# Chunk products of an mLSTM from fp32r high and low parts in place of plain fp32

## The chip, the cores and the metric

One core of one Trainium2 chip. The time is device microseconds (us) of one execution of the whole layer. The engines are called PE (TensorE), ACT (ScalarE), DVE (VectorE), POOL (GpSimd) and SP (SyncE, which issues nearly all DMAs).

## What is computed

A hybrid layer on 1024 tokens of width 1024, all in fp32: RMS norm, one wide input projection, a causal convolution, an mLSTM branch (4 heads of 256, chunks of 128 tokens), a dilated attention branch, two output projections with gates, a last projection and norm. The change is in the mLSTM recurrence, which per head and chunk of 128 tokens is

```python
C_new = decay * C + einsum('lk,lv->kv', w * k, v)        # state, 256 x 256
n_new = decay * n + einsum('lk->k', w * k)
s = einsum('ld,sd->ls', q, k) * exp(log_d - m_t)          # scores of the chunk
num = inter * (q @ C_prev) + s @ v
den = inter * (q @ n_prev) + s.sum(-1)
h = num / maximum(abs(den), exp(-m_t))
```

and in the sums that make the input and forget gates (`if_pre`) from the normed x.

## The kernel before, in words

The projections dominate. They are done by a seven-product scheme of Strassen's kind on blocks of x (B11, B21, B22 and the sums T1 to T4) and of the weights; each product is 4 contraction tiles times 3 matmuls, because every fp32 operand is split into an fp32r high part (hi, a rounded copy) and a low part (lo, the rest), and hi*hi, hi*lo and lo*hi are added in PSUM. One product is thus 12 matmuls of 128x512. The program is a hand-written table over steps k = 0, 1, ...; in step k PE does the side work of `items[k]`, then product k. For product k+3 the high part of the weights is made by ACT in step k (`high`, L1456; it waits until product k-1 is done) and the low part by POOL (`low`, L1080), or by DVE for two of seven products (L1887). POOL also makes the sums S1 and S2 of the weights (L1068, L1074) in every seventh step, after which S2 waits for a low part of DVE. DVE and ACT read the products out of PSUM and do the convolution ("taps", L2001, three per tile). Work of a step that comes behind `low` stands in the lists `act_late`, `dve_late`, `pool_late`; each engine works strictly in the order of its program.

The recurrence is side work of PE. Chunk (h, n) is number n of head h. Its start, in items[s] (`chunk_start`), makes the scores (L1317), turns the output gate (L1321), and turns k and v into the PSUM tile `keep` (L1332, L1334). ACT copies v and k (scaled) to `vv` and `kw` (L1721, L1723) and takes the exponential of the decay matrix `dmat` (L1726); DVE multiplies it with the scores into `w` (L2165). Its end, in items[s+2] (`chunk_end`), is up to five fp32 products of 258 columns: A = q times state (two, L1345; not for n = 0), B = w times v (L1350), C = k times v (two, L1354; not for n = 7). DVE then adds A and B, normalises, and updates `state` (L2190). The starts are at step 177 + 3.25 n for head 0, 203 + 4.375 n and 238 + 4.375 n for heads 1 and 2, and 273 + 3.5 n for head 3, rounded down. `keep` and the tiles of PSUM called side are read by order of semaphores; `pe_ring` counts the fills of the side ring.

At the start of the program x comes in eight row tiles; ACT squares five of them (L1508), POOL takes the root (L1092), DVE scales (L2076), PE turns them, ACT makes high parts (L1513) and DVE low parts (L2046) of B11 and B21. The gate sums are two side items: half 0 of the tokens from B11 and B21 (16 matmuls of 128x512 by L1259), half 1 from B11, T1 and B22 (24).

Of the kernel before, what the change touches and what calls it, by code (L numbers as in the profile page):

```python
# [13 lines left out]
P = 128  # L14
DM = 1024
# [26 lines left out]
HM_SLOTS = 12  # L42
# [103 lines left out]
def hybrid_kernel(nc, x, w_in, w_if, w_pm, w_pa, w_out, b_gate, conv_wt, conv_bt, pre_wt, m_wt, post_w,  # L146
# [94 lines left out]
    chunks = sorted(start_of, key=lambda c: start_of[c])  # L241
    for h, n in chunks:
        s = start_of[h, n]
# [100 lines left out]
    for s in range(NSTEP):  # L344
        for it in items[s]:
            what = it[0]
            if what == "if":
                fill(("if", it[1]), "act")
# [50 lines left out]
    with ctx:  # L399
# [65 lines left out]
        hm_sb = at("hm_sb", [P, HM_SLOTS, MD], F32, A_Q)  # L465
# [7 lines left out]

        state = small("state", [P, 2, VE], F32)
        kw_sb = [small(f"kw{i}", [P, MD], F32) for i in range(2)]
        vv_sb = [small(f"vv{i}", [P, VE], F32) for i in range(2)]
        w_sb = [small(f"w{i}", [P, P], F32) for i in range(2)]
        o_gate = [small(f"o_gate{i}", [P, MD], F32) for i in range(2)]
        dmat = small("dmat", [P, P], F32)
        total = small("total", [P, VE], F32)  # L480
        sq_junk = small("sq_junk", [P, MD], BF16, 2)
# [47 lines left out]
        ifw = small("ifw", [P, KT, 2 * MH], F32)  # L529
        assert pos[0] <= nc.sbuf_usable_end, (pos[0], nc.sbuf_usable_end)  # L530
# [51 lines left out]
        x2_in = [sem(f"x2_in{i}") for i in range(4)]  # L582
# [7 lines left out]
        pe_y = sem("pe_y")  # L590

        x_sq = sem("x_sq")
# [6 lines left out]
        ring_act = sem("ring_act")  # L599
        keep_act = sem("keep_act")  # L600
# [5 lines left out]
        e_done, kv_done, sq_done = sem("e_done"), sem("kv_done"), sem("sq_done")  # L606
        m_norm = sem("m_norm")
        att_hi, hm_hi, w_out_hi = sem("att_hi"), sem("hm_hi"), sem("w_out_hi")
        ysq_done, mg_hi = sem("ysq_done"), sem("mg_hi")

        v_step = sem("v_step")
        x_ms, x_sq_late, x_scaled = sem("x_ms"), sem("x_sq_late"), sem("x_scaled")
# [160 lines left out]
        def _(sp):  # L773
# [95 lines left out]
            def piece(it):  # L869
# [9 lines left out]
                elif what == "if_out":  # L879
                    ring_taken(sp, ("if", 1))  # L880
# [152 lines left out]
            def x_again(t):  # L1033
# [4 lines left out]
                sp.dma_start(gst[t % 4][:], x[t * P:(t + 1) * P, :]).then_inc(x2_in[t % 4], 16)  # L1038
# [19 lines left out]
        def _(g):  # L1058
# [28 lines left out]
            def reciprocal_root(t):  # L1087
                if t < 5:
                    g.wait_ge(x_ms, t + 1)
                else:  # L1090
                    g.wait_ge(x_sq_late, t - 4)
                TT(ssq[:, NT + t:NT + t + 1], ssq[:, t:t + 1], halfneg[:, 0:1], ALU.pow).then_inc(x_rs, 1)  # L1092

            def diagonal(t):
                reciprocal_root(t)
                g.wait_ge(x_rs, t + 1)
# [6 lines left out]
            for t in range(4):  # L1103
                reciprocal_root(t)
            reciprocal_root(4)
            low(0)
# [13 lines left out]
            for k in range(NSTEP):  # L1120
# [1190 lines left out]
```

## Time and profile before

| | |
|---|---|
| median of 3 runs | 1369.98 us (1368.76 to 1371.14) |
| the profiled execution | 1369.94 us, its span 1368.1 us |
| PE busy | 1352.3 us, 99% of the span |
| DVE, ACT, POOL busy | 794.5, 641.7, 569.2 us (58, 47, 42%) |
| PE's share of the chain that ended last | 91% |

The busy times of matmuls overlap (a record lasts longer than the distance to the next), so the cost of a matmul on PE is read from start to start in the order of time. A plain fp32 product is two records; an fp32r product, or a transpose, is one.

### The profile page before, as it was taken

How to read it: one execution, taken by the hardware profiler on the slowest of the kernel's cores; microseconds unless marked ns; L12 is line 12 of the kernel's file. 1: busy time of each engine (PE TensorE's matmuls, PEld its weight loads, DVE VectorE, ACT ScalarE, POOL GpSimd, SP SyncE). 2: the span in 40 equal slices, each digit the busy share in tenths (PEclk: the TensorE clock that was granted, in tenths of full speed). 3: DMA queues.
4: the chain of work that ended last, by engine and by line, in shares of the span. 5: the costliest groups of instructions: out<-in, count | busy, mean ns of one | idle time of the engine just before them, and what ended most of it. 6: DMA issues, size and time to landing. Idle time of an engine off the chain costs nothing.

```text
span 1368.1 us, 18779 instructions
## 1 busy us (share of the span) xinstructions
PE 1352.3 (99%) x6470; PEld 1127.3 (82%) x6470; DVE 794.5 (58%) x1260; ACT 641.7 (47%) x1320; POOL 569.2 (42%) x400
## 2 busy tenths in 40 slices
PE   7999999999999999999999999999999999999998
PEld 5788888888888888888888888888888888888786
DVE  5874438346543835877756575755644442997632
ACT  6644543543444455345445445544544553533421
POOL 5253435335443534654434445344333544454000
PEclk9999999999999999999999999999999999999999
DMA  6132233324233323455442634345343354966421
GB/s 194 51 76 65 69 74 90 96 48 126 76 85 72 84 79 61 149 173 144 114 145 66 188 104 134 100 127 175 87 150 97 93 188 165 345 200 196 183 97 58
DMA packets 210462, 165.02 MB, mean 121 GB/s; under 512 B 32400, under 2 KB 186544, under 8 KB 210368
## 3 DMA queue, kind: packets, MB, share of 16 engines
q1 hardware_dynamic: 210224, 163.75, 40.5%
q8 instruction: 53, 0.87, 0.3%
q14 instruction: 41, 0.34, 0.1%
q10 hardware_dynamic: 144, 0.07, 0.0%
HBM read 117.41 MB, written 40.08 MB: 115 GB/s over the span
## 4 chain that ended last, share of the span: by engine, by line
PE 91%; DVE 4%; issue 2%; ACT 1%; DMA 1%; SPq 1%; POOL 0%; DVEq 0%; POOLq 0%; ACTq 0%
PE proj L1244 69%; PE side L1189 3%; PE proj L1189 2%; PE side L1289 2%; PE side L1268 2%; PE side L1345 2%; PE side L1354 2%; PE proj L1170 2%; PE side L1170 2%; PE side L1277 1%; PE side L1317 1%; PE side L1350 1%; PE side L1300 1%; DMA x_sb<-x_in 1%; PE side L1362 1%
## 5 line engine op out<-in xcount | busy, mean ns | idle before, releaser
L1080 POOL TENSOR_TENSOR w_lo<-raw,w_hi 128x512 fp32r<-128x512 f32 x161 | 234.5, 1458 | 413.8 <-ACT w_hi L1456 413.7
L1244 PE MATMUL proj<-hi_T,w_hi 128*128 128x512 f32 x832 | 338.1, 406 | 2.2 <-ACT snap L1474 1.6
L1244 PE MATMUL proj<-hi_T,w_lo 128*128 128x512 f32 x832 | 325.2, 391 | 0.0
L1244 PE MATMUL proj<-lo_T,w_hi 128*128 128x512 f32 x832 | 324.1, 390 | 0.0
L1244 PE MATMUL proj<-hi_B,w_hi 128*128 128x512 f32 x624 | 254.1, 407 | 5.6 <-ACT b_sb L1518 4.0
L1244 PE MATMUL proj<-hi_B,w_lo 128*128 128x512 f32 x624 | 244.2, 391 | 0.0
L1244 PE MATMUL proj<-lo_B,w_hi 128*128 128x512 f32 x624 | 243.6, 390 | 0.0
L1080 POOL TENSOR_TENSOR w_lo<-s_sb,w_hi 128x512 fp32r<-128x512 f32 x104 | 156.7, 1510 | 153.5 <-ACT w_hi L1456 153.4
L1244 PEld LDWEIGHTS proj<-hi_T,w_hi 128*128 128x128 f32 x832 | 156.4, 188 | 36.0 <-issue 3.5
L1244 PEld LDWEIGHTS proj<-hi_T,w_lo 128*128 128x128 f32 x832 | 156.1, 188 | 34.2
L1244 PEld LDWEIGHTS proj<-lo_T,w_hi 128*128 128x128 f32 x832 | 156.6, 188 | 30.4
L1456 ACT ACTIVATE w_hi<-raw 128x512 fp32r<-128x512 f32 x216 | 135.2, 627 | 70.5 <-PE proj L1244 57.6
L1244 PEld LDWEIGHTS proj<-hi_B,w_hi 128*128 128x128 f32 x624 | 117.7, 189 | 29.9 <-ACT b_sb L1518 4.2
L1244 PEld LDWEIGHTS proj<-hi_B,w_lo 128*128 128x128 f32 x624 | 117.4, 188 | 25.4
L1244 PEld LDWEIGHTS proj<-lo_B,w_hi 128*128 128x128 f32 x624 | 117.8, 189 | 22.8
L1074 POOL TENSOR_TENSOR s_sb<-s_sb,raw 128x512 f32<-128x512 f32 x52 | 82.9, 1594 | 91.3 <-DVE w_lo L1887 90.5
L1456 ACT ACTIVATE w_hi<-s_sb 128x512 fp32r<-128x512 f32 x156 | 97.7, 627 | 37.9 <-PE proj L1244 28.9
L1887 DVE TENSOR_TENSOR w_lo<-s_sb,w_hi 128x512 fp32r<-128x512 f32 x52 | 43.9, 845 | 85.5 <-ACT w_hi L1456 85.5
L1068 POOL TENSOR_TENSOR s_sb<-raw 128x512 f32<-128x512 f32 x52 | 75.5, 1453 | 21.5 <-DVE w_lo L1887 21.4
L2001 DVE SCALAR_TENSOR_TENSOR tmp<-stage,cw,tmp 128x1023 f32<-128x1023 f32 (+2 forms) x48 | 76.1, 1585 | 0.7
L2144 DVE CUSTOM_DVE_ANT_0 prob<-side,mask_sb 128x128 f32<-128x128 f32 (+1 forms) x96 | 29.2, 347 | 67.3 <-PE side L1268 67.2
L1474 ACT ACTIVATE snap<-proj 128x512 f32<-128x512 f32 x52 | 31.1, 597 | 78.0 <-PE proj L1244 77.9
(253 smaller groups left out, 2014.5 us busy)
## 6 DMA issues: line engine op xcount, KB each, us to landing
raw<-w_in SPq DMA_DIRECT2D x95, 512.0 KB, 6.0
m_spill<-stage SPq DMA_DIRECT2D x16, 1024.0 KB, 5.6
chunk<-m_spill SPq DMA_DIRECT2D x32, 512.0 KB, 3.8
gate_spill<-stage SPq DMA_DIRECT2D x8, 1024.0 KB, 4.3
gst<-gate_spill SPq DMA_DIRECT2D x32, 256.0 KB, 3.2
share<-share_spill SPq DMA_DIRECT2D x12, 512.0 KB, 5.0
x_sb<-x_in SPq DMA_DIRECT2D x8, 512.0 KB, 7.6
hm_spill<-stage SPq DMA_DIRECT2D x4, 1024.0 KB, 8.8
```

Source lines behind the costliest of these rows:

```text
L1068: ins = TT(s1_sb[:], a21, a22, ALU.add)
L1074: ins = TT(s2_sb[:], s1_sb[:], a11, ALU.subtract)
L1080: TT(w_lo_ring[k % RING][:], src, w_hi_ring[k % RING][:].bitcast(F32), ALU.subtract).then_inc(lo_pool, 1)
L1170: mm = pe.matmul(pa_slot(t)[:, tokens], w[:, kt, :], m[:, kt, tokens], start=(kt == 0 and w is wh and m is at_hi), stop=(kt == AH - 1 and ...
L1189: mm = pe.matmul(y_slot(t)[:, columns], a[:, kt, :], w[i][:, j, columns], start=(kt == 0 and a is hi_part and w is out_hi), stop=(kt == KT ...
L1244: mm = pe.matmul(acc(p, which), w[:, kt, :], m[:, kt, :], start=(first and kt == 0 and w is wh and m is h_hi[b]), stop=(kt == 3 and w is w ...
L1268: mm = pe.matmul(b[:, at_ * P:(at_ + m) * P], qo_sb[(NG * h + g) % 4][:, n * P:(n + 1) * P], k_sb[g][:, (n + 1 - m) * P:(n + 1) * P], star ...
L1456: A(w_hi_ring[k % RING][:], src, ACT.Copy).then_inc(hi_done, 1)
L1474: A(snap[0][:], a, ACT.Copy).then_inc(u3_done, 1)
L1887: TT(w_lo_ring[k % RING][:], operand(p, weight_name(k)), w_hi_ring[k % RING][:].bitcast(F32), ALU.subtract).then_inc(lo_dve, 1)
L2001: ins = STT(t_[:, d:], src[:, 0:S - d], cw[:, t, 3 - d:4 - d], t_[:, d:], ALU.mult, ALU.add)
L2144: ins = V.tensor_tensor_reduce(out=prob_part(h, i)[:, part], in0=b[:, part], in1=mask, scale=-ASCALE, scalar=3.0e38, op0=ALU.add, op1=ALU. ...
```

## The change

1. **Parts.** All chunk products but the scores are made as three fp32r products from high and low parts. ACT makes the high parts: of q (`q_hi`), of w (`cw_hi`), of the state (`state_hi`), and v and k directly (`vv_hi`, `kw_hi`). DVE makes `vv_lo` and `kw_lo` in `chunk_start`, ahead of w. POOL makes `q_lo` and `cw_lo` behind the `low` of step s+1, and `state_lo` behind that of the step after the end. k, v, w parts and the output gate have one buffer now instead of two.
2. **The end** of a chunk stands in items[s+3] instead of items[s+2] where the next chunk starts more than three steps after this one: in 22 of 32 chunks.
3. **Gates.** The four B11 tiles of the sum (8 matmuls) are issued in step 2, copied aside by ACT for half 1, and go on with B21 in step 4; half 1 leaves B11 out and DVE adds the copy.
4. **The start.** The square and the scaling of row tile 4 stand behind the first two high parts and the first three low parts; POOL makes the first w_lo ahead of the root of tile 4.
5. Ten instead of twelve slots for the head's output (`hm_sb`), and semaphores merged.

```diff
-HM_SLOTS = 12
+HM_SLOTS = 10
...
-    items[2].append(("if", 0))
+    items[2].append(("if_top",))
+    items[4].append(("if", 0))
     items[8].append(("if", 1))
-    act_late[2].append(("if", 0))
-    act_late[8].append(("if", 1))
+    act_late[4].append(("if", 0))
+    dve_late[9].append(("if", 1))
...
+    end_of = {}
+    for c, at_ in enumerate(chunks):
+        s = start_of[at_]
+        end_of[at_] = s + (2 if c + 1 < len(chunks) and start_of[chunks[c + 1]] <= s + 3 else 3)
...
-        free = start_of[chunks[c - 2]] + 2 if c > 1 else 171
+        free = end_of[chunks[c - 2]] if c > 1 else 171
...
-        items[s + 2].append(("end", h, n))
-        act_late[s + 3].append(("square", h, n))
+        items[e].append(("end", h, n))
+        act_late[s + 1].append(("w_high", h, n))
+        pool_late[s + 1].append(("parts", h, n))
+        act_late[e + 1].append(("square", h, n))
+        if n < NT - 1:
+            act_late[e + 1].append(("state_high", h, n))
+            pool_late[e + 1].append(("state", h, n))
...
+                    if what == "parts":
+                        if n:
+                            g.wait_ge(q_high, later_no(h, n))
+                            g.wait_ge(pe_ring, ring_no["qk", h, n] + 1)
+                            TT(q_lo[c % 2][:], chunk_sb[c % 2][:, 0:2, :], q_hi[:].bitcast(F32), ALU.subtract
+                               ).then_inc(q_low, 1)
+                        g.wait_ge(w_high, c + 1)
+                        TT(cw_lo[:], dmat[:], cw_hi[:].bitcast(F32), ALU.subtract).then_inc(w_done, 1)
+                    elif what == "state":
+                        g.wait_ge(state_high, (NT - 1) * h + n + 1)
+                        TT(state_lo[:], state[:], state_hi[:].bitcast(F32), ALU.subtract).then_inc(state_done, 1)
...
+            def three_products(into, w, m):
+                for i, (a, b) in enumerate(((0, 0), (0, 1), (1, 0))):
+                    mm = pe.matmul(into, w[a], m[b], start=(i == 0), stop=(i == 2))
...
                 if n:
-                    ring_taken(pe, ("C", h, n - 1, 1))
+                    pe.wait_ge(q_low, later_no(h, n))
+                    pe.wait_ge(state_done, later_no(h, n))
                     for d in range(2):
-                        mm = pe.matmul(keep[:, 0:VE], chunk_sb[c % 2][:, d, :], state[:, d, :],
-                                       start=(d == 0), stop=(d == 1))
+                        for a, m in ((q_hi, state_hi), (q_hi, state_lo), (q_lo[c % 2], state_hi)):
+                            mm = pe.matmul(keep[:, 0:VE], a[:, d, :], m[:, d, :],
+                                           start=(d == 0 and a is q_hi and m is state_hi), stop=(d == 1 and a is not q_hi))
                     mm.then_inc(pe_keep, 1)
-                ring_taken(pe, ("qk", h, n))
+                pe.wait_ge(w_done, c + 1)
...
+                elif what == "w_high":
+                    ring_taken(act, ("qk", h, n))
+                    if c:
+                        act.wait_ge(pe_ring, ring_no["B", *divmod(c - 1, NT)] + 1)
+                    A(cw_hi[:], dmat[:], ACT.Copy).then_inc(w_high, 1)
...
+                dve.wait_ge(kv_hi, c + 1)
+                ins = TT(vv_lo[:, 0:MD], keep[:, MD:2 * MD], vv_hi[:, 0:MD].bitcast(F32), ALU.subtract)
+                if n < NT - 1:
+                    ins = STT(kw_lo[:], keep[:, 0:MD], cols[:, 2, h, n:n + 1], kw_hi[:].bitcast(F32), ALU.mult, ALU.subtract)
+                ins.then_inc(kv_done, 1)
```

POOL in the stretch of chunks (0,0) and (0,1), before (`w_lo` are the low parts of weights, `s_sb` the sums S1 and S2):

```order
L1080 TENSOR_TENSOR w_lo_76<-raw_68,w_hi_72 128x512
L1068 TENSOR_TENSOR s_sb<-raw_67 128x512
L1074 TENSOR_TENSOR s_sb<-s_sb,raw_67 128x512
L1080 TENSOR_TENSOR w_lo_78<-raw_67,w_hi_74 128x512
L1080 TENSOR_TENSOR w_lo_75<-s_sb,w_hi_71 128x512
L1080 TENSOR_TENSOR w_lo_76<-s_sb,w_hi_72 128x512
```

and after the change:

```order
L1105 TENSOR_TENSOR w_lo_76<-raw_68,w_hi_72 128x512
L1162 TENSOR_TENSOR cw_lo<-dmat,cw_hi 128x128
L1093 TENSOR_TENSOR s_sb<-raw_67 128x512
L1099 TENSOR_TENSOR s_sb<-s_sb,raw_67 128x512
L1105 TENSOR_TENSOR w_lo_78<-raw_67,w_hi_74 128x512
L1166 TENSOR_TENSOR state_lo<-state,state_hi 128x516
L1105 TENSOR_TENSOR w_lo_75<-s_sb,w_hi_71 128x512
L1159 TENSOR_TENSOR q_lo_132<-chunk_123,q_hi 128x256
L1162 TENSOR_TENSOR cw_lo<-dmat,cw_hi 128x128
L1105 TENSOR_TENSOR w_lo_76<-s_sb,w_hi_72 128x512
```

The low part of the state of chunk (0,0) now stands between two w_lo, and q_lo and cw_lo of chunk (0,1) behind the second. PE at the end of chunk (0,1), before:

```order
L1345 MATMUL side<-state,chunk_123 128x258 x2
L1350 MATMUL side<-vv_131,w_133 128x258
L1354 MATMUL side<-vv_131,kw_129 128x258 x2
```

and after:

```order
L1401 MATMUL side<-state_hi,q_hi 128x258
L1401 MATMUL side<-state_lo,q_hi 128x258
L1401 MATMUL side<-state_hi,q_lo_132 128x258
L1401 MATMUL side<-state_hi,q_hi 128x258
L1401 MATMUL side<-state_lo,q_hi 128x258
L1401 MATMUL side<-state_hi,q_lo_132 128x258
L1388 MATMUL side<-vv_hi,cw_hi 128x258
L1388 MATMUL side<-vv_lo,cw_hi 128x258
L1388 MATMUL side<-vv_hi,cw_lo 128x258
```

with six more of L1388 for C behind them. Five fp32 products have become fifteen of fp32r, and the first of them wait for `state_lo` and `q_lo`.

## Rows read from the trace of the kernel before

**Rows 1.** The page, shares of the span.
```profile
PE 1352.3 (99%) x6470; PEld 1127.3 (82%) x6470; DVE 794.5 (58%) x1260; ACT 641.7 (47%) x1320; POOL 569.2 (42%) x400
```
**Rows 2.** The page, the chain that ended last, by engine.
```profile
PE 91%; DVE 4%; issue 2%; ACT 1%; DMA 1%; SPq 1%; POOL 0%; DVEq 0%; POOLq 0%; ACTq 0%
```
**Rows 3.** Waits of PE (us, times, longest), and one stretch (busy PE, PEld, DVE, ACT, POOL, PEclk).
```profile
PE proj L1244 <- ACT b_sb L1518: 4.0, 1, 4.0
PE proj L1244 <- DVE lo_B L2046: 1.6, 2, 0.8
...
650.00:700.00 50.00, 50.00 (x242) 42.23 (x241) 34.82 (x58) 25.10 (x55) 18.77 (x14) 1.00 0.41 122
```
**Rows 4.** PE in order of time (start us, length us): chunks (0,0), (0,1), (0,5).
```profile
619.68 0.59 PE L1350 MATMUL side<-vv,w 128*128 128x258 f32 x2
...
624.39 0.38 PE L1332 MATMUL side<-ident,chunk 128*128 128x128 f32 x2
624.61 0.38 PE L1334 MATMUL side<-ident,chunk 128*128 128x128 f32 x2
...
627.57 0.39 PE L1244 MATMUL proj<-hi_T,w_hi 128*128 128x512 f32 x1
...
630.30 1.03 PE L1345 MATMUL side<-state,chunk 128*128 128x258 f32 x4
631.17 0.60 PE L1350 MATMUL side<-vv,w 128*128 128x258 f32 x2
...
679.07 1.03 PE L1345 MATMUL side<-state,chunk 128*128 128x258 f32 x4
```
**Rows 5.** Groups of PE by line (records | busy us, mean ns).
```profile
L1354 PE MATMUL side<-vv,kw 128*128 128x258 f32 x112 | 28.9, 381 | 0.0
L1345 PE MATMUL side<-state,chunk 128*128 128x258 f32 x112 | 28.9, 379 | 0.0
```
**Rows 6.** The start in order of time, DVE and PE, and one stretch with its granted clock.
```profile
11.35 0.75 DVE L2076 TENSOR_SCALAR x_sb<-x_sb,ssq 128x1024 f32<-128x1024 f32 x1 [0.66 <-POOL ssq L1092]
...
14.05 1.74 DVE L2076 TENSOR_SCALAR x_sb<-x_sb,ssq 128x1024 f32<-128x1024 f32 x1 [0.66 <-POOL ssq L1092]
...
17.23 0.80 PE L1244 MATMUL proj<-hi_B,w_hi 128*128 128x512 f32 x1 [3.98 <-ACT b_sb L1518]
...
16.70:20.10 3.40, 2.87 (x7) 2.29 (x8) 2.73 (x4) 3.40 (x7) 0.02 (x1) 0.50 1.19 290
```
**Rows 7.** ACT in order of time around chunk (0,1).
```profile
626.93 0.62 ACT L1456 ACTIVATE w_hi<-raw 128x512 fp32r<-128x512 f32 x1
...
627.86 0.19 ACT L1656 ACTIVATION_READ_ACCUMULATOR sq_junk<-hm_sb,rden 128x1 f32 x1
```
**Rows 8.** POOL and DVE in order of time around chunks (0,0) and (0,1).
```profile
616.40 4.09 POOL L1080 TENSOR_TENSOR w_lo<-raw,w_hi 128x512 fp32r<-128x512 f32 x2 [6.04 <-ACT w_hi L1456]
...
627.63 1.87 POOL L1080 TENSOR_TENSOR w_lo<-raw,w_hi 128x512 fp32r<-128x512 f32 x1 [2.06 <-ACT w_hi L1456]
629.46 2.25 POOL L1080 TENSOR_TENSOR w_lo<-s_sb,w_hi 128x512 fp32r<-128x512 f32 x1
632.78 1.29 POOL L1080 TENSOR_TENSOR w_lo<-s_sb,w_hi 128x512 fp32r<-128x512 f32 x1 [1.08 <-ACT w_hi L1456]
...
612.40 1.28 DVE L2001 SCALAR_TENSOR_TENSOR tmp<-stage,cw,tmp 128x1023 f32<-128x1023 f32 x1
...
627.07 5.72 DVE L2001 SCALAR_TENSOR_TENSOR tmp<-stage,cw,tmp 128x1023 f32<-128x1023 f32 x3
```
**Rows 9.** Rows nearest to the new small copies, POOL and DVE.
```profile
25.41 0.61 POOL L1097 TENSOR_SCALAR diag<-ident,ssq 128x128 f32<-128x128 f32 x1
...
632.82 0.49 DVE L2172 SCALAR_TENSOR_TENSOR total<-side,cols,total 128x258 f32<-128x258 f32 x1
```
**Rows 10.** POOL in order of time around chunk (0,5).
```profile
676.52 2.12 POOL L1074 TENSOR_TENSOR s_sb<-s_sb,raw 128x512 f32<-128x512 f32 x1 [3.75 <-DVE w_lo L1887]
678.61 1.72 POOL L1080 TENSOR_TENSOR w_lo<-raw,w_hi 128x512 fp32r<-128x512 f32 x1
```

More of the change, by code:

```diff
@@ L474, in hybrid_kernel @@
         state = small("state", [P, 2, VE], F32)
[L475 to L479, printed above, removed]
+        state_hi = small("state_hi", [P, 2, VE], F32R)
+        state_lo = at("state_lo", [P, 2, VE], F32R, A_P + 26112)
+        q_hi = small("q_hi", [P, 2, P], F32R)
+        q_lo = [at(f"q_lo{i}", [P, 2, P], F32R, A_P + 16896 + i * 4608) for i in range(2)]
+        kw_hi, kw_lo = small("kw_hi", [P, MD], F32R), small("kw_lo", [P, MD], F32R)
+        vv_hi, vv_lo = small("vv_hi", [P, VE], F32R), small("vv_lo", [P, VE], F32R)
+        cw_hi, cw_lo = small("cw_hi", [P, P], F32R), small("cw_lo", [P, P], F32R)
+        o_gate = small("o_gate", [P, MD], F32)
+        dmat = at("dmat", [P, P], F32, A_P + 26112 + 2112)
         total = small("total", [P, VE], F32)
-        sq_junk = small("sq_junk", [P, MD], BF16, 2)
         assert pos[0] <= A_P + 12800, pos[0] - A_P
@@ L1247, in product, with gate_tokens @@
                 mm.then_inc(pe_prod, 1)
-            def gate_tokens(half):
-                b = work(("if", half))
-                if half == 0:
-                    pe.wait_ge(iw_lo_done, 1)
-                    parts = [(kt, name) for name, o in (("B11", 0), ("B21", 4)) for kt in range(o, o + 4)]
-                else:
-                    parts = [(kt, name) for name, o in (("B11", 0), ("T1", 0), ("B22", 4)) for kt in range(o, o + 4)]
+            def gate_tokens(b, parts, first, last):
                 for i, (kt, name) in enumerate(parts):
@@ L1258, in gate_tokens, with gate_top_rows, gate_half @@
                     for m in (h_hi[name], h_lo[name]):
-                        mm = pe.matmul(b[:], iw[:, kt, :], m[:, kt % 4, :], start=(i == 0 and m is h_hi[name]),
-                                       stop=(i == len(parts) - 1 and m is h_lo[name]))
+                        mm = pe.matmul(b, iw[:, kt, :], m[:, kt % 4, :], start=(first and i == 0 and m is h_hi[name]),
+                                       stop=(last and i == len(parts) - 1 and m is h_lo[name]), skip_group_check=True)
+                return mm
+            def gate_top_rows():
+                copied(pe, 2)
+                pe.wait_ge(iw_lo_done, 1)
+                gate_tokens(bank[0], [(kt, "B11") for kt in range(4)], True, False).then_inc(pe_gate, 1)
+            def gate_half(half):
+                b = work(("if", half))
+                if half == 0:
+                    pe.wait_ge(gate_top, 1)
+                    mm = gate_tokens(b, [(kt, "B21") for kt in range(4, 8)], False, True)
+                else:
+                    mm = gate_tokens(b, [(kt, name) for name, o in (("T1", 0), ("B22", 4)) for kt in range(o, o + 4)],
+                                     True, True)
                 mm.then_inc(pe_ring, 1)
```

162 lines of the change are left out of this document (99 added, 63 removed).

## The prediction

> **What bounds the kernel now.** I read the page's shares first, then the chain, then TensorE's waits, then the order of time on each engine around a chunk. TensorE (PE) is busy 99% of the span [rows 1] and makes 91% of the chain that ended last [rows 2]. Its longest wait is 4.0 us, once, at the start; the DVE waits are 1.6 us [rows 3]. From 650 to 700 us, amid the chunk recurrence (613 to 1049 us), it has no gap at all, at a granted clock of 1.00 [rows 3], and none of its listed waits lies in that stretch. So a product removed from TensorE is worth its interval, and a late operand there costs its lateness in full, since nothing before the change fills such a hole. The edit does both: it shortens the work of TensorE and makes every chunk product wait for more steps of ScalarE and GpSimd.
>
> **Prices on TensorE.** Busy times overlap, so I take start-to-start intervals. Plain fp32 products of 258 columns are two records each: four records of L1345 from 630.30 to 631.17 [rows 4] are two products, 0.435 us each. There are 112 records of A, 112 of C [rows 5] and two of B in each of 32 chunks: 288 records, 144 products, 62.6 us. The change makes 3 x 144 = 432 fp32r products of 258 columns. No row has this shape. The nearest is the fp32r product of 512 columns, started every 0.227 us (twelve in 2.72 us, [rows 4]). Bounds: in proportion to columns 0.114 us; or 258 columns at 2.4 GHz, 0.1075 us, plus the 0.0134 us by which 512 columns exceed their own 0.2133 us, together 0.121 us. I take 0.121, since a fixed share per instruction is the likelier reading: 52.3 us. Gain 10.3 us (13.4 at the other bound).
>
> The gate sums over block B11 are made once and reused: 8 products of 512 columns fewer, 8 x 0.227 = 1.8 us. They are issued where TensorE is busy, apart from up to 0.8 us of waits for the low parts of T2, whose cover (the second four pairs of if) moves two products later.
>
> **The start.** On ScalarE the first high part stands behind the square of x row tile 4, and DVE scales that tile for 1.74 us before the first low part [rows 6]. Both move behind. TensorE's first block then waits for the chain of low parts on DVE, for which TensorE waited twice, 1.6 us in all [rows 3]. That chain starts some 2.5 us earlier, but takes in the scale (0.75 us for another tile, [rows 6]), squares and lows as before: about 1.0 us earlier at its end. Of this I keep 0.8 us, because behind it DVE makes the low parts of the T blocks at nearly TensorE's pace. Bounds 0 and 1.6 (the whole 1.6 us that TensorE waited for lo_B). Sum of the gains: 10.3 + 1.8 + 0.8 = 12.9 us.
>
> **What the chunk products now wait for.** Per chunk ScalarE adds q_hi (128x256), cw_hi (128x128) and state_hi (128x516); the nearest row is 0.62 us for 128x512 [rows 7], and at 47% ScalarE has room for the 1.1 us that they come to. DVE adds vv_lo and kw_lo, some 0.49 us each (the read of 128x258 from PSUM, [rows 9]); they lie before the 5.4 us of two products and cost nothing there. GpSimd adds state_lo, as large as w_lo: 1.29 us; q_lo, half as wide: 0.65 us by columns; cw_lo 0.33 us by columns, 0.61 us by the nearest 128x128 row [rows 9]. I take 0.65 and 0.4. That is 2.3 us more GpSimd work per chunk on an engine busy 42% [rows 1]: mean load is no limit, its place in the queue is.
>
> On GpSimd, q_lo and cw_lo stand behind the w_lo of the step after the chunk's start, and that w_lo starts only when ScalarE has made w_hi after TensorE has finished one product. Take chunk (0,1). Its end products are due at 630.30 [rows 4]. GpSimd makes w_lo at 627.63 (1.87 us) and 629.46 (2.25 us), back to back, while DVE makes three taps [rows 8]. In the new order state_lo of chunk (0,0) comes between them and q_lo behind both. Undisturbed: 629.5 + 1.29 + 1.28 + 0.65 = 632.7, so 2.5 us late. But GpSimd and DVE hold each other up here: three taps of 1.28 us took 5.72 us and two copies of 1.28 us took 4.1 us. With the third tap taking its turn inside this queue it is 635.0, 4.8 us late. ScalarE's state_hi is ready before (w_hi at 626.93, the square to 628.05, then 0.62: 628.7, [rows 7]). I take 4.4.
>
> Chunk (0,5) is alike: s_sb ends at 678.64 [rows 10], then state_lo, w_lo, q_lo give 681.9, or 683.0 with one tap between, against 679.07 [rows 4]: 2.8 to 4.0, I take 3.7. Chunk (0,0) has no q_lo, but its second w_lo ends at 620.49 [rows 8] and cw_lo behind it at 620.9, against 619.68 [rows 4]: 1.2 us, and 0.1 for the semaphore.
>
> The same sum over all 32 chunks: an end two products after its start remains in ten chunks (six of head 0, four of head 3); of the other three of head 0, (0,2) and (0,4) are 0.4 us late, (0,6) 0.9. In head 3 even steps leave w_lo to DVE and GpSimd is free: nothing. In the 22 chunks whose end moves a product later there are 2.72 us more, which covers all but three, where the two sums for s_sb (1.3 and up to 2.1 us) or a state_lo stand ahead: (1,1), (2,1) and (3,1), 1.0 us each. Sum of the smaller ones: 4.7 us. Together 1.3 + 4.4 + 3.7 + 4.7 = **14.1 us** of new waits; from 8.4 (no blocking by taps) to 19 (full turns, every marginal chunk late).
>
> **Edits at nothing.** Ten instead of twelve hm slots: the transposes that free a slot stand before the chunk end that needs it by table (hmT of head 0 at step 211, chunk (1,2) ends at 214). Single buffers for kw, vv and o_gate: the last user is done before the next start, since a later end is chosen only where the next start leaves room. The chunk load moves a product later in places and still has four products, 10.9 us, before its use. If DVE's backlog breaks one of these, TensorE waits at a chunk start. Merged semaphores and moved junk buffers change no order.
>
> **Sum.** The profiled execution took 1369.9 us, as the median of the three runs (1369.98). 1369.9 - 12.9 + 14.1 = **1371 us**. About 0.2%, 2.7 us, is what a measurement of this kernel can tell from no change; so the forecast is no change, with a lean to slower.
>
> **Rivals.**
> 1. *GpSimd keeps up.* The taps yield, w_lo runs at 1.28 us, and DVE's own extra work spreads the collisions. Waits of about 5 us: 1369.9 - 12.9 + 5 = 1362. For it: most w_lo in these stretches do take 1.28 us, and 32 chunks have 13 us of time each. Against it: state_lo and q_lo are serial behind the w_lo in two chunks even without a collision (5.3 us).
> 2. *Half clock behind the long waits* (slower). After 3.98 us without work TensorE's clock stood at 0.50 (1.2 GHz) from 16.7 to 20.1 us [rows 6]: 1.7 us of work lost. The two long waits are near that length. Where a wait reaches about 4 us, each costs 1.7 us more, and as GpSimd then blocks DVE longer, (3,1), (1,1), (2,1) and the chunks at the margin (five with q_lo within 0.2 us of its time) get late as well: waits 16.5, plus 3.4: 1369.9 - 12.9 + 19.9 = 1377. It decides from waits over 15.6 us.
> 3. *Loads of weights aren't hidden under short products.* Then a product of 258 columns takes its 0.1075 us plus a load. A 128-column transpose with its load starts every 0.11 us [rows 4], which bounds a load; 432 x 0.217 = 94 us against 62.6, with the waits 1369.9 - 2.6 + 31 + 14 = 1412, less if the waits hide in it. Against it: 512 columns stream in 0.213 us and start every 0.227, so a load of up to 0.11 us is nearly all hidden. The Trainium skill (TensorE: Matmul & The Clock Gate, Part 3, "What overlaps and what doesn't") says that a weight load overlaps a running matmul only when their row groups differ; all products here use the whole array. By that rule the change loses this much; this case's trace disagrees with it at 512 columns.
> 4. *The edit of the gates and the start brings nothing*: the eight products come back as waits for low parts of T2 and T1, with TensorE at DVE's pace. 1371 + 2.6 = 1374.
>
> **How the numbers follow.** Forecast 0.42, rival 1 0.27, rival 2 0.24, rival 3 0.03, rival 4 0.04. The forecast's own range is 1367 to 1375: of its 0.42 some 0.28 lies within 0.2%, 0.12 above, 0.02 below. Rival 1 gives 0.26 to faster and 0.01 to no change; rival 4 0.01 to no change and 0.03 to slower. Faster 0.28, same 0.30, slower 0.42. The range runs from rival 1's time less the other bound of a product's price in part (1361) to rival 2's with two more marginal chunks (1379).
>
> **What would show it.** Right: L1388 and L1401 of the new kernel start every 0.12 us; TensorE has waits for GpSimd (q_lo, state_lo, cw_lo) with the two longest at chunks (0,1) and (0,5), 3 to 5 us, and nearly none in heads 1 to 3; GpSimd is busy about 70 us more; the gate's rows fall from 40 products to 32. Wrong: intervals far from 0.12; waits for GpSimd spread over all chunks or absent; TensorE waiting for DVE (kw_lo) or for a chunk's load; a clock under 1.00 between 600 and 1050 us without long waits.

## The result: 2.5% slower, and the profile after

The changed kernel takes **1404.54 us** (median of 4 runs, 1402.42 to 1408.58), the kernel before 1369.76 (4 runs on the same chip, 1368.76 to 1371.14). The ratio is 1.0252, with an interval of 1.0240 to 1.0265. The forecast was 1371, its range ended at 1379. The profiled execution took 1402.42 us, its span is 1400.2.

The page of the changed kernel, shares of the span and the chain that ended last, against [rows 1, 2]:

```profile
PE 1350.8 (96%) x6606; PEld 1127.7 (81%) x6606; DVE 840.1 (60%) x1321; ACT 670.0 (48%) x1408; POOL 671.1 (48%) x488
...
PE 75%; POOL 8%; DVE 5%; issue 4%; ACT 2%; DMA 1%; SPq 0%; DVEq 0%; POOLq 0%; ACTq 0%
```

PE has 136 records more, as the edit says (288 become 432, 8 fewer in the gates), and is busy 1.5 us less; but the span grew by 32.1 us, and 8% of the chain is now POOL's. POOL gained 101.9 us of busy time, where the prediction said 70: q_lo, cw_lo and state_lo come to 31.2, 21.6 and 41.1 us. The new time of the span is idle time of PE. PE's waits, for the whole span (us, times, longest), against [rows 3]:

```profile
PE side L1401 <- POOL q_lo L1159: 30.3, 18, 4.5
...
PE side L1388 <- POOL cw_lo L1162: 1.7, 1, 1.7
```

The first line is the result: 18 chunks wait for `q_lo`, 30.3 us. Read over the stretches of the program (windows: us, then busy PE, PEld, DVE, ACT, POOL, granted clock, DMA share, GB/s), the chunk recurrence of the changed kernel looks like this; 613 to 1132 is its whole length, then comes 650 to 700, which the prediction had singled out, and three short stretches:

```profile
613.00:1132.00 519.00, 486.69 (x2488) 411.51 (x2487) 340.88 (x557) 274.35 (x600) 313.16 (x232) 0.99 0.38 114
...
650.00:700.00 50.00, 40.53 (x214) 34.56 (x213) 30.15 (x50) 23.00 (x52) 29.17 (x24) 0.97 0.41 119
...
634.80:641.70 6.90, 4.60 (x19) 4.39 (x20) 1.92 (x6) 2.16 (x4) 3.74 (x4) 0.52 0.24 71
696.30:699.70 3.40, 3.24 (x16) 3.27 (x17) 0.46 (x1) 0.90 (x2) 0.31 (x1) 0.53 0.08 20
959.10:962.50 3.40, 3.29 (x16) 3.32 (x17) 1.31 (x3) 1.30 (x4) 1.92 (x2) 0.52 0.00 0
```

and in the kernel before, the same stretch:

```profile
613.00:1100.60 487.60, 487.60 (x2345) 410.55 (x2344) 294.76 (x498) 245.81 (x513) 210.31 (x144) 1.00 0.41 121
```

Before, PE had no idle time at all between the first scores of chunk (0,0) and the last transposes of the recurrence. After, 32.3 of 519 us are idle, and 13.7 us run at a granted clock of about 0.5 (1.2 GHz). Taken between the same two events (613.11 to 1100.66 before, 613.54 to 1132.38 after) the stretch grew from 487.55 to 518.83 us, by **31.3 us**; ahead of it 0.4 us were lost, behind it 0.4. So the whole loss lies in the recurrence. PE around the end of chunks (0,0) and (0,1), in order of time (start us, length us), against [rows 4]:

```profile
622.25 0.28 PE L1388 MATMUL side<-vv_hi,cw_lo 128*128 128x258 f32 x1
622.37 0.28 PE L1388 MATMUL side<-vv_hi,kw_hi 128*128 128x258 f32 x1
...
632.20 0.39 PE L1283 MATMUL proj<-hi_T,w_lo 128*128 128x512 f32 x1
637.10 0.55 PE L1401 MATMUL side<-state_hi,q_hi 128*128 128x258 f32 x1 [4.52 <-POOL q_lo L1159]
637.45 0.42 PE L1401 MATMUL side<-state_lo,q_hi 128*128 128x258 f32 x1
637.67 0.42 PE L1401 MATMUL side<-state_hi,q_lo 128*128 128x258 f32 x1
```

At full clock a new product starts every 0.12 us, as priced (the median over all chunks is 0.121). Chunk (0,1) starts its end at 637.10 instead of 632.43 (one interval of 0.227 behind 632.20): 4.7 us late, and then each product takes 0.22 us, since the clock has fallen. What POOL and DVE did before that, against [rows 8]:

```profile
629.80 1.95 POOL L1105 TENSOR_TENSOR w_lo<-raw,w_hi 128x512 fp32r<-128x512 f32 x1 [2.06 <-ACT w_hi L1514]
631.72 2.25 POOL L1166 TENSOR_TENSOR state_lo<-state,state_hi 128x516 fp32r<-128x516 f32 x1
633.93 2.23 POOL L1105 TENSOR_TENSOR w_lo<-s_sb,w_hi 128x512 fp32r<-128x512 f32 x1
636.13 0.72 POOL L1159 TENSOR_TENSOR q_lo<-chunk,q_hi 128x256 fp32r<-128x256 f32 x1
...
629.33 5.71 DVE L2081 SCALAR_TENSOR_TENSOR tmp<-stage,cw,tmp 128x1023 f32<-128x1023 f32 x3
```

This is the chain that the prediction drew: three operations of POOL, each lengthened from 1.3 to about 2 us beside DVE's three taps, and `q_lo` behind them. The same view at chunk (0,5), where w_lo and q_lo stand behind state_lo, and at (1,6), which the prediction had on time:

```profile
692.83 1.71 POOL L1105 TENSOR_TENSOR w_lo<-raw,w_hi 128x512 fp32r<-128x512 f32 x1
694.50 1.70 POOL L1159 TENSOR_TENSOR q_lo<-chunk,q_hi 128x256 fp32r<-128x256 f32 x1
...
829.94 2.26 POOL L1105 TENSOR_TENSOR w_lo<-s_sb,w_hi 128x512 fp32r<-128x512 f32 x1
832.16 1.70 POOL L1159 TENSOR_TENSOR q_lo<-chunk,q_hi 128x256 fp32r<-128x256 f32 x1
```

`q_lo` takes 1.70 us there, against 0.65 in the prediction. Over all 28 of them (the answer for the tile; ns min/median/max, first and last start):

```profile
L1159 POOL TENSOR_TENSOR q_lo<-chunk,q_hi x28: 716/1176/1705, 636.1 to 1081.7; 128x256 fp32r<-128x256 f32 x28
```

### The profile page after: what moved, and what is told of

The parts are those of the page before. It is cut to its first block, busy times and chain, and to the rows that moved or that the text cites. A ratio compares the mean times of both kernels' runs of the same rounds, so it can differ in the third digit from the quotient of the medians.

```text
span 1400.2 us, 19459 instructions
## 1 busy us (share of the span) xinstructions
PE 1350.8 (96%) x6606; PEld 1127.7 (81%) x6606; DVE 840.1 (60%) x1321; ACT 670.0 (48%) x1408; POOL 671.1 (48%) x488
## 4 chain that ended last, share of the span: by engine, by line
PE 75%; POOL 8%; DVE 5%; issue 4%; ACT 2%; DMA 1%; SPq 0%; DVEq 0%; POOLq 0%; ACTq 0%
PE proj L1283 56%; POOL w_lo L1105 3%; PE side L1228 3%; PE proj L1228 2%; PE side L1337 2%; PE side L1316 2%; PE side L1388 2%; DVE tmp L2081 2%; PE side L1401 2%; POOL q_lo L1159 2%; POOL s_sb L1099 1%; PE side L1325 1%; POOL state_lo L1166 1%; POOL s_sb L1093 1%; ACT w_hi L1514 1%
## 5 line engine op out<-in xcount | busy, mean ns | idle before, releaser
L1105 POOL TENSOR_TENSOR w_lo<-raw,w_hi 128x512 fp32r<-128x512 f32 x161 | 245.2, 1524 | 338.1 <-ACT w_hi L1514 338.1
L1283 PE MATMUL proj<-hi_T,w_hi 128*128 128x512 f32 x832 | 334.7, 402 | 3.5 <-ACT snap L1532 1.6
L1093 POOL TENSOR_TENSOR s_sb<-raw 128x512 f32<-128x512 f32 x52 | 78.4, 1507 | 21.8 <-DVE w_lo L1967 21.8
L2081 DVE SCALAR_TENSOR_TENSOR tmp<-stage,cw,tmp 128x1023 f32<-128x1023 f32 (+2 forms) x48 | 83.1, 1732 | 0.7
```

What stands on the lines that cost most here:

```text
L1093: ins = TT(s1_sb[:], a21, a22, ALU.add)
L1105: TT(w_lo_ring[k % RING][:], src, w_hi_ring[k % RING][:].bitcast(F32), ALU.subtract).then_inc(lo_pool, 1)
L1283: mm = pe.matmul(acc(p, which), w[:, kt, :], m[:, kt, :], start=(first and kt == 0 and w is wh and m is h_hi[b]), stop=(kt == 3 and w is w ...
L2081: ins = STT(t_[:, d:], src[:, 0:S - d], cw[:, t, 3 - d:4 - d], t_[:, d:], ALU.mult, ALU.add)
```

## The experiments

A, B and C are the products q times state, w times v, k times v. Each was timed against the kernel before on the same chip (1370.3 to 1371.3 us there); experiments 5 and 7 have two executions each, the others four to twelve. Differences to the changed kernel go across chips, where the kernel before differed by up to 1.6 us. "The recurrence" is the stretch between the two events above, 487.55 us before and 518.83 after.

**1. The gates and the start alone.** The kernel before with parts 3 and 4 of the change and the merged semaphores of part 5 (the slots stay twelve), cut:

```diff
-    items[2].append(("if", 0))
+    items[2].append(("if_top",))
+    items[4].append(("if", 0))
...
-    act_late[2].append(("if", 0))
-    act_late[8].append(("if", 1))
+    act_late[4].append(("if", 0))
+    dve_late[9].append(("if", 1))
```

and the square and the scaling of row tile 4 behind the first parts, as in the change.

> The kernel before with the edits of the gates and the start alone (chunk products plain fp32, ends where they were). In the trace of the changed kernel the first product of the chunk region comes 0.46 us later than before, although TensorE begins 1.3 us earlier. Theory A (the eight products saved come back as waits for low parts at the pace of DVE, and a second stretch at half clock): 1369.5 to 1370.5, no difference. Theory B (the prediction's term): 2.6 us faster, 1367.2.

Measured: 1372.7 us, ratio 1.0011 (1.0002 to 1.0020). The part that the prediction put at -2.6 us brings nothing, if anything it costs a little. Its waits of PE and the granted clock at its start (columns as above):

```profile
PE proj L1251 <- ACT b_sb L1536: 2.3, 1, 2.3
PE proj L1389 <- DVE x_sb L2099: 1.7, 2, 1.0
PE proj L1251 <- DVE lo_B L2069: 1.7, 3, 0.8
```

```profile
15.80:22.60 6.80, 6.00 (x14) 4.29 (x15) 5.61 (x8) 6.34 (x12) 3.77 (x4) 0.52 0.95 225
26.10:29.50 3.40, 3.40 (x14) 2.81 (x13) 0.46 (x3) 2.14 (x6) 3.02 (x3) 0.55 0.00 0
```

PE waits less for its first operand (2.3 us; 4.0 in [rows 3], 5.1 in experiment 2, which has the old start), then it waits for x tiles and low parts, and there is a second stretch at half clock, here of 3.4 us. The first stretch proves nothing: with the old start it took 3.4 us in the kernel before and in experiment 10, and 6.8 us in experiments 2, 9 and 11. The second one is in every kernel with the new start and in none with the old.

**2. The later ends alone.** The kernel before with part 2 only:

```diff
+        end_of[at_] = s + (2 if c + 1 < len(chunks) and start_of[chunks[c + 1]] <= s + 3 else 3)
...
-        items[s + 2].append(("end", h, n))
+        items[e].append(("end", h, n))
```

> The kernel before with the ends of 22 chunks one product later and nothing else. All theories: plain products have their operands early, so no change within 1 us (1369 to 1371). If it is slower by more than 2 us, the place of the ends alone costs, by the chunk loads or the reads out of PSUM.

Measured: 1371.38 us, ratio 1.0002 (0.9993 to 1.0012). Where the ends stand costs nothing as long as the products are plain.

**3. The changed kernel with all ends early.** All 32 stand two products after their start again.

```diff
-        end_of[at_] = s + (2 if c + 1 < len(chunks) and start_of[chunks[c + 1]] <= s + 3 else 3)
+        end_of[at_] = s + 2
```

> The changed kernel with all ends two products after the start. Theory E (a later end takes a product from the way of the state to the next chunk, which is what makes (0,4) late; the move costs more than it gives): at most 1404, perhaps 1398. Theory Q (the waits come from where q_lo and cw_lo stand in GpSimd's queue, and in the 22 chunks the extra product hides 2.72 us of it): 22 chunks with up to 2.7 us more each, those now late by their full 2.7, so 1404 + 8 to + 45: 1415 to 1450.

Measured: 1455.3 us, ratio 1.0612 (1.0596 to 1.0628): 51 us more than the changed kernel. PE's longest entry:

```profile
PE side L1401 <- POOL q_lo L1159: 58.9, 21, 4.9
```

So the step by which 22 ends move is what keeps the change from costing 6%, and the clock takes its share too. The recurrence takes 568.6 us, 49.8 more than in the changed kernel. PE is idle for 61.4 us of it instead of 32.3. The other 20.7 us are PE's busy time with the same products, as 61.4 us run at about half clock here (14 stretches) against 13.7.

**4. Without DVE's taps.** The changed kernel, but DVE leaves out the three shifted taps of the convolution, except for one column of the last; so most of the convolution is missing, to see the collision of DVE and POOL alone.

```diff
                     for d in which:
-                        ins = STT(t_[:, d:], src[:, 0:S - d], cw[:, t, 3 - d:4 - d], t_[:, d:], ALU.mult, ALU.add)
-                        if d < 3:
-                            step(ins)
-                        else:
+                        if d == 3:
+                            ins = STT(t_[:, d:d + 1], src[:, 0:1], cw[:, t, 3 - d:4 - d], t_[:, d:d + 1], ALU.mult, ALU.add)
```

> The changed kernel with the convolution's three shifted taps left out on DVE (one column remains of the last), 48 operations of 1.3 to 1.9 us with two SBUF inputs; the result of the convolution is then not the reference's. Theory L (waits are made by GpSimd's copies being held up by these): q_lo takes 0.72 us in nearly all chunks, waits in chunks (0,0), (0,1), (0,4), (0,5), (1,6), (2,6) fall by 1.5 to 2.5 us each and the stretches at half clock go: 1404 - 12 - 5 = 1387. Theory Q (queue place alone, taps hardly matter): 1400 to 1404. DVE's own time isn't on TensorE's way in either theory.

Measured: 1383.41 us, ratio 1.0090 (1.0076 to 1.0104), 21 us less than the changed kernel. PE's waits for q_lo and the tile q_lo on POOL:

```profile
PE side L1401 <- POOL q_lo L1159: 15.1, 14, 3.3
```

```profile
L1159 POOL TENSOR_TENSOR q_lo<-chunk,q_hi x28: 716/752/1196, 634.5 to 1063.0; 128x256 fp32r<-128x256 f32 x28
```

The median q_lo falls from 1.18 to 0.75 us and the longest from 1.71 to 1.20: the difference is DVE's taps. Half of the waits remain, though. Chunk by chunk, the lateness of (1,3), (2,3), (1,6) and (2,6) is gone (1.9 and 2.4 us each in the changed kernel), that of (0,4) falls from 3.8 to 1.2 and that of (0,1) from 4.7 to 2.1 us. But (0,2), (3,1) and eight chunks with 0.6 to 1.0 us are late by the same as before, within 0.01 us. One of these is (1,4), and POOL and DVE ahead of its end show why:

```profile
786.23 1.74 POOL L1093 TENSOR_TENSOR s_sb<-raw 128x512 f32<-128x512 f32 x1
789.34 1.20 POOL L1159 TENSOR_TENSOR q_lo<-chunk,q_hi 128x256 fp32r<-128x256 f32 x1
...
785.28 1.54 DVE L1967 TENSOR_TENSOR w_lo<-s_sb,w_hi 128x512 fp32r<-128x512 f32 x1 [1.68 <-ACT w_hi L1514]
788.51 1.44 DVE L1958 TENSOR_TENSOR raw<-raw 128x512 f32<-128x512 f32 x1
```

The sum and q_lo have the lengths that they have in the changed kernel (1.74 and 1.17 us) and are longer than alone (1.28 and 0.72) by 0.9 us, with DVE's other operations of two SBUF inputs beside them. The taps make a part of the hold-up, not all of it.

**5. q_lo one place earlier.** It moves into POOL's list of the chunk's own step, ahead of the next w_lo.

```diff
-        pool_late[s + 1].append(("parts", h, n))
+        pool_late[s].append(("q_part", h, n))
+        pool_late[s + 1].append(("parts", h, n))
```

> The changed kernel with q_lo in GpSimd's list of the chunk's first step instead of the second (everything else as it is). Theory Q (queue place): A no longer waits for q_lo where state_lo is early; B then waits for cw_lo, which ends where it ended less the 0.7 us of q_lo, and has 0.7 us more by A's six products. Each late chunk is late by about 1.4 us less: 36 us of waits fall to about 16, and half clock to one or two stretches: 1380 to 1386. Theory L (being held up by DVE counts, not the place): q_lo meets DVE in the first step as well, gain under 10 us.

Measured: 1393.42 us, ratio 1.0163 (1.0136 to 1.0191), 11 us less than the changed kernel. PE's waits:

```profile
PE side L1392 <- POOL cw_lo L1166: 12.4, 13, 1.7
PE side L1405 <- POOL q_lo L1160: 8.4, 7, 3.3
```

The last operand in the queue is cw_lo now, and the wait passes to it. Neither theory had the number: PE's idle time in the recurrence fell from 32.3 to 21.0 us, near the 16 of theory Q, but 20.5 us of it ran at half clock instead of 13.7, in three stretches where Q had expected one or two.

**6. POOL's new operations ahead of its old ones in each step.**

```diff
             for k in range(NSTEP):
-                if k and k + LEAD < NK and not low_dve[k + LEAD]:
-                    low(k + LEAD)
...
                 for it in pool_late[k]:
...
+                if k and k + LEAD < NK and not low_dve[k + LEAD]:
+                    low(k + LEAD)
```

> The changed kernel with GpSimd's q_lo, cw_lo and state_lo ahead of the w_lo and the sums S1 and S2 of the same step. Theory Q: cw_hi is there about 5 us after the chunk's start, so cw_lo ends at 5.5 to 6.5, before the end at 6.6 or 9.3; nearly all waits for GpSimd's parts go (under 5 us left), and with 10.3 us less work on TensorE it is 1369.8 - 10.3 + 5 = 1362 to 1367, unless w_lo now comes late for its product (which has 8 us of room). Theory L: waits stay, since each copy is held up by DVE as before; over 1385.

Measured: 1401.65 us, ratio 1.0224 (1.0207 to 1.0241), hardly better. POOL in order of time at chunk (0,1):

```profile
632.65 2.25 POOL L1161 TENSOR_TENSOR state_lo<-state,state_hi 128x516 fp32r<-128x516 f32 x1 [3.08 <-ACT state_hi L1724]
634.86 2.23 POOL L1105 TENSOR_TENSOR w_lo<-raw,w_hi 128x512 fp32r<-128x512 f32 x1
```

Here POOL idles for 3.1 us, since state_lo, now ahead, waits for a state that ACT has not yet turned into state_hi; then w_lo and q_lo stand behind it as before. Theory Q's 1362 to 1367 is far off, and the 1385 of theory L is met for another reason than it gave. Neither of the two orders tried is good for all of the list: what is made last (the state) and what is due first (q_lo) share one queue. An order with q_lo early and state_lo late was not tried.

**7. q_lo by DVE.** It stands behind the multiplication with the scores.

```diff
                 TT(dmat[:], bank[i % BANKS][:, 0:P], dmat[:], ALU.mult).then_inc(ring_dve, 1)
+                if n:
+                    dve.wait_ge(q_high, later_no(h, n))
+                    TT(q_lo[c % 2][:], chunk_sb[c % 2][:, 0:2, :], q_hi[:].bitcast(F32), ALU.subtract).then_inc(q_low, 1)
```

> The changed kernel with q_lo made by DVE behind w in the chunk's start instead of by GpSimd. Theory Q: as with q_lo early, 1380 to 1386, or less, as GpSimd's queue is shorter by 0.7 to 1.7 us per chunk for the state too: 1376. Theory L: DVE takes two SBUF inputs once more, and blocks GpSimd instead: over 1390.

Measured: 1386.5 us, ratio 1.0113 (1.0093 to 1.0133), 18 us less. DVE takes 0.41 us for it where POOL took 1.18 in the median. What remains:

```profile
PE side L1383 <- POOL cw_lo L1157: 14.2, 10, 2.5
PE side L1396 <- POOL state_lo L1161: 2.9, 2, 1.9
```

**8. A stays plain.** The changed kernel without q_hi, q_lo, state_hi, state_lo:

```diff
-                        for a, m in ((q_hi, state_hi), (q_hi, state_lo), (q_lo[c % 2], state_hi)):
-                            mm = pe.matmul(keep[:, 0:VE], a[:, d, :], m[:, d, :],
-                                           start=(d == 0 and a is q_hi and m is state_hi), stop=(d == 1 and a is not q_hi))
+                        mm = pe.matmul(keep[:, 0:VE], chunk_sb[c % 2][:, d, :], state[:, d, :],
+                                       start=(d == 0), stop=(d == 1))
```

> The changed kernel with q times state left plain fp32 (no q and state parts at all; B and C from parts). TensorE saves 88 products of 0.435 less 264 of 0.12: 6.6 us. Only cw_lo is then made by GpSimd. Theory Q: it stands where q_lo stood, behind w_lo, but GpSimd's queue has 2.0 us per chunk less, and A's 0.87 us run ahead of B: waits left in (0,0), (0,1), (0,5) and a few more, 4 to 8 us: 1366 to 1371. If the waits stay near 36 us, they aren't made by q_lo and state_lo: over 1390.

Measured: 1373.77 us, ratio 1.0020 (1.0011 to 1.0029). Its recurrence takes 488.97 us, and PE waits there for one thing:

```profile
PE side L1376 <- POOL cw_lo L1154: 5.3, 3, 2.0
```

This is the run that settles which part costs the time: **A from parts costs 30.8 us** (1404.5 less 1373.8), though its 56 products are 0.435 - 3 x 0.12 = 0.075 us shorter each, 4.2 us in all. All the rest of the change comes to +3, of which the gates and the start are some 1.3. The waits are within the 4 to 8 us expected, the time is not: B and C from parts save 6.6 us of products, and the waits and one stretch of 3.4 us at half clock take all of it back (the recurrence is 1.4 us longer than before).

**9. B and C from parts without POOL.** The kernel before (its start, gates and ends), with B and C from parts, and part 5 and the single buffers of the change; ACT makes cw_hi and DVE cw_lo within the chunk's start:

```diff
                 TT(dmat[:], bank[i % BANKS][:, 0:P], dmat[:], ALU.mult).then_inc(ring_dve, 1)
+                dve.wait_ge(w_high, c + 1)
+                TT(cw_lo[:], dmat[:], cw_hi[:].bitcast(F32), ALU.subtract).then_inc(w_done, 1)
```

> The kernel before, gates, start and ends as they were, with B and C from parts and A plain, and nothing made by GpSimd: ScalarE makes cw_hi right behind the output gate, DVE cw_lo right behind it in the chunk's start. By the runs so far: 88 products of 0.435 become 264 of 0.121, 6.4 us less on TensorE, parts ready some 4 us after a start that has 6.6, no waits and no half clock: ratio 0.9953, 1364.5. If DVE or ScalarE come late by blocking each other, or GpSimd is held up by DVE's extra operations until w_lo is late: over 1369.

Measured: 1369.77 us, ratio 0.9987 (0.9978 to 0.9997). The recurrence takes 484.89 us: 2.7 us less, where 6.4 were due. PE at the start of chunk (0,2), and DVE before it:

```profile
638.91 0.44 PE L1331 MATMUL side<-ident,chunk 128*128 128x128 f32 x2 [1.31 <-DVE state L2223]
```

```profile
630.85 0.29 DVE L2198 TENSOR_TENSOR cw_lo<-dmat,cw_hi 128x128 fp32r<-128x128 f32 x1 [0.38 <-ACT cw_hi L1759]
631.05 5.73 DVE L2029 SCALAR_TENSOR_TENSOR tmp<-stage,cw,tmp 128x1023 f32<-128x1023 f32 x3
...
638.38 0.87 DVE L2223 SCALAR_TENSOR_TENSOR state<-state,decay,side 128x258 f32<-128x258 f32 x2
```

The new copies push the taps back, and the state behind them becomes late. The taps here start 15.8 us behind the start of the recurrence; in the kernel before it is 14.0 (627.07 in [rows 8]), in experiment 11 14.7. PE's waits are 2.0 us for DVE's state and 0.7 for ACT's copy of `total`. The prediction had put DVE's copies at nothing.

**10. All three from parts, again without POOL:** experiment 9 with A as well, q_lo and state_lo by DVE.

```diff
+                    dve.wait_ge(state_high, (NT - 1) * h + n + 1)
+                    TT(state_lo[:], state[:], state_hi[:].bitcast(F32), ALU.subtract).then_inc(state_done, 1)
```

> As the other, and A from parts too: q_lo by DVE behind w, state_hi by ScalarE in the end's own step, state_lo by DVE right behind the state. 144 products become 432: 10.3 us less, ratio 0.9925 (1360) if no wait appears. Theory L (DVE and GpSimd hold each other up): the two more DVE operations with two SBUF inputs lengthen the w_lo of GpSimd, yet these have 8 us of room. The state's chain is 6.3 us behind the end of a chunk, the next is 10.6 away. A wait for state_lo in head 0 would show it wrong: 1362 to 1368.

Measured: 1377.69 us, ratio 1.0045 (1.0031 to 1.0060), the recurrence 494.85 us. PE's waits:

```profile
PE side L1333 <- DVE state L2239: 6.2, 4, 2.6
...
PE side L1365 <- DVE q_lo L2210: 2.7, 4, 0.8
```

Adding A costs 8 us over experiment 9. Through POOL it costs 31 (experiment 8), so DVE carries it some 23 us cheaper, in kernels that also differ in their ends and in who makes cw_lo. The expectation's 1360, and the 1362 to 1368 with a wait, both missed: PE is idle for 13.1 us of the recurrence, 11.7 of them for DVE's state, ACT's `total` and q_lo.

**11. C alone from parts.** The kernel before; A and B stay plain, ACT makes vv_hi and kw_hi (and a plain copy of v for B), DVE vv_lo and kw_lo. Part 5 and the single buffers of the change are in it as well, which no run tested alone. (The expectation calls C the product of weights and values: it is that of the weighted keys and the values, L1354 before; "the high parts of weights" are kw_hi.)

```diff
-                        pe.matmul(b[:, 0:VE], kw_sb[c % 2][:, d * P:(d + 1) * P], v, start=True, stop=True
-                                  ).then_inc(pe_ring, 1)
+                        three_products(b[:, 0:VE], (kw_hi[:, keys], kw_lo[:, keys]), v).then_inc(pe_ring, 1)
```

> The kernel before with only the product of weights and values (C) from high and low parts: ScalarE makes the high parts of weights and values, VectorE the low ones; the products with keys and queries stay plain fp32, GpSimd's list and all steps are those of before. By rows: 56 products x (0.435 - 0.363 us) = 4.1 us less on TensorE, so about 1366 to 1367 us, ratio 0.997, if VectorE's copy of the state comes in time now that cw_lo is gone from its queue (theory: VectorE's load in the chunk's start was what ate 3.7 of the 6.4 us in the run with B and C from parts). Rival: the wait for the state's copy behind VectorE's filter taps is not of cw_lo's making, then that wait (about 1.3 us in a chunk, 2 us in all) and waits for w_lo stay, 1369 to 1370 us, ratio 0.999 to 1.000.

Measured: **1367.23 us, ratio 0.9976 (0.9967 to 0.9985)**, a little faster than the kernel before. The window over its recurrence:

```profile
613.00:1099.00 486.00, 485.82 (x2413) 411.88 (x2411) 319.66 (x562) 255.09 (x546) 215.88 (x144) 1.00 0.42 122
```

PE waits there once, for 0.2 us. The recurrence takes 483.45 us, 4.1 less than before, which is the whole of 56 x (0.435 - 0.363). The median gained 3.0. Where the other 1.1 us are is open. The profiled execution was the longest of the eleven (1371.99, 4.8 above the median). Behind the recurrence it has a wait of 2.2 us for DVE, which ends at 1175.90, and a stretch at half clock from 1176.7 to 1180.1, some 1.7 us of work lost; in the kernel before neither is there. Whether the other executions have them can't be seen.

## Why the prediction was wrong, point by point

- **What bounds the kernel: right.** PE had no slack in the recurrence, and each late operand showed in the end time in full.
- **The price of a product: right.** 0.12 us measured, 0.121 taken; the gain of 10.3 us is there. Experiment 11 measured 4.1 us for 56 products, as the same prices give. Rival 3 (loads of weights not hidden) fell with the same rows, and with it the rule of the Trainium skill (TensorE: Matmul & The Clock Gate, Part 3, "What overlaps and what doesn't"): this trace disagrees with it at 258 columns too.
- **The gates and the start: wrong, rival 4 was right.** Taken as -2.6 us, measured as 1.3 us slower (interval 0.3 to 2.7) in experiment 1. The earlier begin was bought with new waits and with a second stretch at half clock. Of rival 4's mechanism, waits for low parts of T, 0.6 us is seen (1.1 us against 0.5 in experiment 2); the rest are x tiles and the clock.
- **The three large waits: right.** (0,0), (0,1), (0,5) were 1.8, 4.7 and 4.4 us late, 10.9 together, against 1.3 + 4.4 + 3.7 = 9.4. (The 2.5 us undisturbed at (0,1) are 2.4 by the prediction's own sum; without the taps experiment 4 has 2.1.)
- **The smaller ones: this is the step that failed.** "Sum of the smaller ones: 4.7 us" measured about 25 us (from start to start over all chunks: 35.6 in all, less 10.9). Two things were missing. First, ACT's order. (0,2), (0,4) and (0,6) were put at 0.4, 0.4 and 0.9 us and came at 1.8, 3.8 and 1.8. The prediction gave ACT's copies a load ("room for the 1.1 us") but a place only at (0,1). At (0,4) DVE has the state ready at 670.6, and ACT makes `state_hi` 3.4 us later, since in its list it stands behind the next chunk's copies of v and k and a w_hi; at (0,2) it is 4.5 us. DVE, ACT and POOL in order of time at (0,4):

```profile
669.73 0.86 DVE L2283 SCALAR_TENSOR_TENSOR state<-state,decay,side 128x258 f32<-128x258 f32 x2
...
674.01 0.64 ACT L1722 ACTIVATE state_hi<-state 128x516 fp32r<-128x516 f32 x1
...
674.73 2.00 POOL L1166 TENSOR_TENSOR state_lo<-state,state_hi 128x516 fp32r<-128x516 f32 x1 [5.20 <-ACT state_hi L1722]
676.69 2.24 POOL L1105 TENSOR_TENSOR w_lo<-raw,w_hi 128x512 fp32r<-128x512 f32 x1
678.89 1.70 POOL L1159 TENSOR_TENSOR q_lo<-chunk,q_hi 128x256 fp32r<-128x256 f32 x1
```

  POOL had nothing to do for 5.2 us and then did it all too late. This lateness is not handed on from the chunk before: (0,2) is 1.76 us late both where (0,1) is 4.7 late and where it is 2.1 (experiment 4), and (0,3), ahead of (0,4), is on time. With (0,3)'s end, and so its state_hi, one product earlier (experiment 3), (0,4) is 1.6 us late instead of 3.8. No run moved state_hi alone.

  Second, the lengths beside DVE. The 2.72 us more of the later ends, "which covers all but three", did not: (1,6) and (2,6) were 2.4 us late, (1,3), (2,3) and (3,1) 1.8 to 1.9, eight others 0.6 to 1.0 (among them (3,4) and (3,6), whose ends stand two products after the start); (1,1) and (2,1), which the prediction had named, were on time. There the list is copies or sums and q_lo, and each was priced undisturbed (1.28 and 0.65). They took 1.7 to 2.3 and 1.2 to 1.7 where DVE worked with two inputs in SBUF. The prediction had seen such turns [rows 8] and charged them in the three large ones only. The taps make the waits of (1,3), (2,3), (1,6), (2,6) and 2.6 of the 3.8 us of (0,4); for the rest, as far as read ((0,2), (1,4), (3,1), (3,3)), DVE's low parts and additions stand beside POOL, and no run took these away. Experiment 4 put 21 us on DVE's taps, experiment 8 put 31 on A.
- **Rival 2, the half clock: right in kind.** Three stretches in the recurrence ran at about 0.5: 11.13 us of busy PE at half speed, so 5.6 us lost by estimate, where 3.4 were priced in two stretches.
- **Edits at nothing.** The later ends: right (experiment 2), and more than that, they saved 51 us (experiment 3). DVE's copies: right for vv_lo and kw_lo, which cost nothing in experiment 11. In experiment 9, with cw_lo among them, 3.7 us of an expected 6.4 were gone; in the change itself cw_lo is POOL's.

Put together for the recurrence: 35.6 - 10.3 + 5.6 = 30.9 us, measured 31.3. The signs against the forecast were those it had named: waits for POOL spread over all heads, and a clock under 1.00. The new waits, 14.1 us in the prediction's sum, measured 35.6, and 20 us of the difference lie in the smaller ones.

What was not isolated is the clock's own cost. The 5.6 us are worked out from the trace; no run removed the half clock and kept the waits.

## What to carry to other kernels

An operand that is split into high and low parts is worth it on a full TensorE only if every part is there in time, so ask it of each product separately: here C, whose operands are ready at the chunk's start, brought its full 4 us within the recurrence, and A, whose operand is the one made last, cost 31. When a queue is long, add it up for each place of the cycle, with the lengths that its operations have beside a busy neighbour, and do so for every engine that hands an operand on, here ACT as well as POOL; mean loads of 48% on both said nothing. And where a step in the order can be moved at no cost, try that first: later ends made up for 51 us.

## What the runs showed that was not expected

- **GpSimd's lengths jump.** The same subtraction of 128x256 takes 0.72 us alone, 1.18 in the median, and 1.70 at most, beside DVE's taps; 128x516 takes 1.29 to 2.28. Without the taps (experiment 4) the 128x256 one has a median of 0.75. The Trainium skill (SBUF — State Buffer, "SBUF: two separate sides") says that DVE with two inputs in SBUF and a GpSimd operation that reads SBUF take a shared port pair as an exclusive lock, for the whole instruction. The trace agrees as far as it goes: in the rows shown the longer lengths stand beside DVE operations with two inputs in SBUF, and those of 1.70 us are gone without the taps.
- **The clock doesn't follow the length of a wait alone.** Windows of the changed kernel (columns as above), behind chunk (0,4), whose end came 3.8 us late at 680.85:

```profile
684.00:690.00 6.00, 6.00 (x33) 5.13 (x32) 4.46 (x9) 3.62 (x11) 2.44 (x3) 1.00 0.22 66
```

  The granted clock was 1.00 there, as in 680 to 684. At 959.21 a shorter wait, of 2.25 us, went with the half clock of the window shown above, as one of 2.2 us did in experiment 11:

```profile
959.21 0.55 PE L1401 MATMUL side<-state_hi,q_hi 128*128 128x258 f32 x1 [2.25 <-POOL q_lo L1159]
```

  So the prediction's "where a wait reaches about 4 us" was no safe bound. Which waits are followed by it stays open.
- **The same work is cheaper on DVE.** The 128x256 subtraction takes 0.41 us there against 0.72 at best on GpSimd, but there it delays what DVE makes next (experiments 9 and 10).
